# Eight experts in one straight line, with an expert's last products behind the next expert's first step

## The reference, cut to what matters

```
def moe_swiglu(h, router_w, w_in, w_out):          # h: 256 tokens x 1024
    logits = h @ router_w                           # 8 experts
    top_vals, top_idx = top_k(logits, 2)
    combine = sum(one_hot(top_idx) * softmax(top_vals))
    for e in range(8):                              # w_in[e]: 1024 x 7168, w_out[e]: 3584 x 1024
        g, u = split(h @ w_in[e], 2)
        out = out + combine[:, e] * ((silu(g) * u) @ w_out[e])
    return out
```

## Time and profile before

| | before |
|---|---|
| median of 3 runs | 2003.32 us (2002.88 to 2005.59) |
| profiled execution | 2006.99 us |
| its span, first to last instruction | 2004.9 us |
| PE busy | 1822.5 us, 91% |
| DVE / ACT busy | 474.2 us / 397.8 us |
| mean granted TensorE clock | 0.95 |

### The profile page before, as it was taken

How to read it: one execution, slowest core, us unless ns; L and a number is a source line. 1 busy time by engine, 2 the same in 40 slices (tenths; PEclk the granted TensorE clock), 3 DMA queues, 4 the chain that set the end, 5 groups by cost and what they waited for, 6 DMA issues and landing times.

```text
span 2004.9 us, 36376 instructions
## 1 busy us (share of the span) xinstructions
PE 1822.5 (91%) x16246; PEld 1078.4 (54%) x16246; DVE 474.2 (24%) x765; ACT 397.8 (20%) x671; POOL 34.9 (2%) x71
## 2 busy tenths in 40 slices
PE   5999889999999799757899998999989999999995
PEld 2744478888888588435445453443534434435343
DVE  3323454222333742644200101001010010010103
ACT  3233333222222521542001101010010100100001
POOL 1000100000000000010000000000000000000000
PEclk8998889999999899967899999999999999999997
DMA  9254452332233141547599898989989989899870
GB/s 374 87 207 170 125 170 76 105 97 93 102 113 110 55 139 43 213 157 296 210 373 340 340 378 314 371 325 343 393 314 349 366 321 388 307 348 373 313 307 23
DMA packets 141170, 477.63 MB, mean 238 GB/s; under 512 B 11168, under 2 KB 35096, under 8 KB 122576
## 3 DMA queue, kind: packets, MB, share of 16 engines
q1 hardware_dynamic: 137344, 467.64, 62.9%
q0 software_dynamic: 3664, 7.48, 1.2%
HBM read 473.96 MB, written 1.13 MB: 237 GB/s over the span
## 4 chain that ended last, share of the span: by engine, by line
PE 83%; DVE 8%; ACT 5%; issue 3%; DMA 1%; DVEq 0%; SPq 0%; ACTq 0%
PE ps L929 80%; DMA w_raw<-in_ada_w_dram 1%; DVE w_lo L1439 1%; PE ps L1353 1%; ACT p L815 1%; ACT w_hi L614 1%; DVE work L1503 1%; DVE row_max L1694 1%; PE ps L1101 1%; DVE residual L1526 1%; DVE work L1522 1%; DVE p L1713 0%; ACT work L630 0%; DVE p L1710 0%; ACT work L649 0%
## 5 line engine op out<-in xcount | busy, mean ns | idle before, releaser
L929 PE MATMUL ps<-w_hi,h_t 128*128 128x512 f32 (+1 forms) x960 | 298.2, 391 | 19.3 <-DVE h_t L1492 7.4
L929 PE MATMUL ps<-w_moe,h_te 128*32 128x256 f32 (+1 forms) x3072 | 259.2, 491 | 14.5 <-DVE residual L1835 14.5
L929 PE MATMUL ps<-w_raw,h_te 128*32 128x256 f32 (+2 forms) x4096 | 252.9, 406 | 0.0
L929 PE MATMUL ps<-h_t,w_hi 128*128 128x512 f32 (+1 forms) x768 | 222.0, 374 | 5.0 <-DVE h_t L1492 5.0
L1439 DVE TENSOR_TENSOR w_lo<-w_raw,w_hi 128x2048 fp32r<-128x2048 f32 x58 | 132.9, 2292 | 351.4 <-ACT w_hi L614 351.0
L929 PEld LDWEIGHTS ps<-w_hi,h_t 128*128 128x128 f32 x960 | 182.9, 193 | 60.2 <-issue 8.1
L929 PEld LDWEIGHTS ps<-w_raw,h_te 128*32 128x32 f32 x4096 | 130.6, 110 | 119.5 <-issue 69.7
L929 PEld LDWEIGHTS ps<-w_moe,h_te 128*32 128x32 f32 x3072 | 97.3, 111 | 168.3 <-issue 122.0
L929 PE MATMUL ps<-w_lo,h_t 128*128 128x512 f32 (+1 forms) x480 | 187.1, 390 | 0.0
L1834 DVE TENSOR_TENSOR residual<-silu_g,ps 128x512 f32<-128x512 f32 (+1 forms) x32 | 19.9, 621 | 660.9 <-ACT silu_g L886 660.9
L614 ACT ACTIVATE w_hi<-w_raw 128x2048 fp32r<-128x2048 f32 x58 | 110.8, 1914 | 328.9 <-PE ps L929 307.3
(11 more groups left out here) (233 smaller groups left out, 1265.1 us busy)
## 6 DMA issues: line engine op xcount, KB each, us to landing
w_moe<-in_expert_in_w_dram SPq DMA_DIRECT2D x96, 1024.0 KB, 5.8
w_raw<-in_expert_in_w_dram SPq DMA_DIRECT2D x64, 1024.0 KB, 6.9
w_raw<-in_ada_w_dram SPq DMA_DIRECT2D x48, 1024.0 KB, 5.6
w_raw<-in_expert_out_w_dram SPq DMA_DIRECT2D x48, 1024.0 KB, 6.7
w_moe<-in_expert_out_w_dram SPq DMA_DIRECT2D x48, 1024.0 KB, 7.7
work<-in_expert_in_w_dram SPq DMA_DIRECT2D x32, 1024.0 KB, 6.8
w_raw<-in_expert_in_w_dram SPq DMA_DIRECT2D x64, 512.0 KB, 6.1
w_raw<-in_ffn_in_w_dram SPq DMA_DIRECT2D x44, 512.0 KB, 4.9
```

Of the source, the lines that this page charges most:

```text
L929: return pe.matmul(out_, l, r, start=first, stop=last, skip_group_check=True)
```

## The change

Three things are done. (1) The list of blocks is now that of the whole round (`ROUND`): the eight in-0 blocks of the first expert (`HEAD`), then seven times a `CYCLE` that begins with in 1 and holds the next expert's in 0 ahead of the expert's own out 3, and a `LAST` cycle without it. SP, PE, ACT and DVE follow this order. (2) In round 0 the cycles are written out one after another on PE, ACT and DVE; SP keeps a loop (six turns). Rounds 1 and 2 keep loops on all engines. (3) The four `combine` products stand behind the blocks 4, 5, 6 and 7 of in 1, and the transposes of `onehot` for the next combine behind block 3 of out 0.

```diff
-EXPERT = [("in", 0, b) for b in range(8)]
+HEAD = step_blocks("in", 0)
+LAST = []
 for s_ in range(1, STEPS):
...
+    LAST += step_blocks("in", s_) + step_blocks("out", s_ - 1)
+CYCLE = LAST + step_blocks("in", 0, 1) + step_blocks("out", STEPS - 1)
+LAST = LAST + step_blocks("out", STEPS - 1)
+EB = len(CYCLE)
+ROUND = HEAD + CYCLE * (NE - 1) + LAST
...
@@ SP
-            with sp.Fori(0, NE - 1) as e:
-                for i in range(RING, EB):
-                    refill(rnd, e, i)
-                for i in range(RING):
-                    refill(rnd, e + 1, i)
-            for i in range(RING, EB):
-                refill(rnd, NE - 1, i)
+            with sp.Fori(0, NE - 2) as e:
+                for n in range(RING, EB + 8):
+                    refill(rnd, e, n, e)
+                for n in range(8, RING):
+                    refill(rnd, e + 1, EB + n, e)
+            for n in range(RING + EB * (NE - 2), len(ROUND)):
+                refill(rnd, (n - 8) // EB, n)
@@ ACT
+                silu(e, 3)
+                if not last:
+                    hte(NE * rnd + e + 2)
+                transposed(e, 3)
+                if not last:
+                    silu(e + 1, 0)
+                yhi(e, last)
+            hte(NE * rnd + 1)
+            silu(0, 0)
+            if rnd:
+                with act.Fori(0, NE - 1) as e:
+                    cycle(e)
+            else:
+                for e in range(NE - 1):
+                    cycle(e)
+            cycle(NE - 1, True)
@@ PE
-                    if (kind, s_, b) == ("in", 0, DK - 1):
-                        pe.wait_ge(y_lo, N + 1)
-                        for n, bank in enumerate((7, 5, 6)):
-                            combine(n, bank)
...
-                    if (kind, s_, b) == ("in", 1, 2):
-                        combine(3, 7)
...
+                    if kind == "in" and s_ == 1 and b >= 4:
+                        if b == 4:
+                            pe.wait_ge(y_lo, N + 1)
+                        if b == 5:
+                            pe.wait_ge(actt_ready, J + 1)
+                        if b == 7:
+                            pe.wait_ge(acc_done, N * 4 + 2)
+                        combine(b - 4, (7, 5, 6, 7)[b - 4])
...
-            with pe.Fori(0, NE) as e:
-                expert(e)
+            pe.wait_ge(hte_ready, NE * rnd + 1)
+            for n in range(8):
+                product(0, n, STEPS * NE * rnd)
+            if rnd:
+                with pe.Fori(0, NE - 1) as e:
+                    cycle(e)
+            else:
+                for e in range(NE - 1):
+                    cycle(e)
+            cycle(NE - 1, True)
@@ DVE
+                product(e, 3)
+                if not last:
+                    product(e + 1, 0)
                 ylo(e)
```

More of the change, by code:

```diff
@@ L61, with step_blocks @@
 N_RAW = B_MOE + ADA_BLOCKS
-EXPERT = [("in", 0, b) for b in range(8)]
+def step_blocks(kind, s_, ahead=0):
+    return [(kind, s_, b, ahead) for b in range(WIDTH[s_] // (128 if kind == "in" else 256))]
+HEAD = step_blocks("in", 0)
+LAST = []
 for s_ in range(1, STEPS):
[L64 to L70, removed]
+    LAST += step_blocks("in", s_) + step_blocks("out", s_ - 1)
[3 more added lines that the diff above has]
+ROUND = HEAD + CYCLE * (NE - 1) + LAST
+assert EB % RING == 0 and len(ROUND) == NE * EB
 assert GROUP * 3 == CAP
@@ L412, in ring, with moe_parts, moe_landed, count @@
         return WMOE[:, r - 2 - RAW, :]
[L414 to L425, removed]
+    def moe_parts(n):
+        return 2 if ROUND[n][:2] == ("in", STEPS - 1) else 1
+    def moe_landed(rnd, e, n):
+        def count(top):
+            return sum(16 * moe_parts(m) for m in range(n % RING, top, RING))
+        return rnd * count(len(ROUND)) + e * (count(8 + 2 * EB) - count(8 + EB)) + count(n + 1)
+    def moe_view(n):
+        kind, s_ = ROUND[n][:2]
         if kind == "out":
-            return ring(i).rearrange("p (j n) -> p j n", j=2)
+            return ring(n).rearrange("p (j n) -> p j n", j=2)
         if s_ < STEPS - 1:
-            return ring(i).rearrange("p (u n) -> p u n", u=2)
-        return ring(i).rearrange("p (k u n) -> p k u n", k=2, u=2)
+            return ring(n).rearrange("p (u n) -> p u n", u=2)
+        return ring(n).rearrange("p (k u n) -> p k u n", k=2, u=2)
     Z_BANK = (6, 3)
@@ L492, in experts @@
                 sp.wait_ge(scores, 16)
[L493 to L495 removed]
+                for n in range(RING):
+                    if 2 <= n < 2 + RAW:
+                        was, j = raw_order[N_RAW - RAW + n - 2]
                         if was == "w":
@@ L901, in yhi, with cycle @@
                 ins.then_inc(y_hi, 1)
-            hte(9 * rnd + 1)
-            with act.Fori(0, NE) as e:
-                silu(e, 0)
+            def cycle(e, last=False):
                 transposed(e, 0)
+                silu(e, 1)
+                transposed(e, 1)
                 act.wait_ge(ptt_ready, NE * rnd + e + 1)
                 act.activation(PTR[0:CAP, :], ps[0:CAP, 7, 0:2 * P], ACT.Copy).then_inc(pt_done, 1)
[L909 to L914, removed]
+                silu(e, 2)
+                transposed(e, 2)
+                silu(e, 3)
[14 more added lines that the diff above has]
+            cycle(NE - 1, True)
         experts(0)
@@ L1355, in transposes, with weights, product @@
                 ins.then_inc(tr_ready, 1)
[L1357 to L1361, removed]
+            def weights(e, n):
+                pe.wait_ge(w_landed[n % RING], moe_landed(rnd, e, n))
+                return moe_view(n)
+            def product(e, n, J):
+                kind, s_, b, ahead = ROUND[n]
+                if kind == "in":
+                    if b == 0:
+                        pe.wait_ge(act_done, FG + J + STEPS * ahead + s_)
+                    w = weights(e, n)
+                    if s_ < STEPS - 1:
+                        ins = in_block(b, w, WIDTH[s_])
+                    else:
+                        for k in range(2):
+                            ins = in_block(2 * b + k, w[:, k, :, :], WIDTH[s_])
+                else:
+                    if b == 0:
+                        pe.wait_ge(actt_ready, J + (s_ + 1))
+                    ins = out_block(s_, b, weights(e, n))
+                ins.then_inc(used, 1)
@@ L1362, in expert, with cycle @@
+            def cycle(e, last=False):
                 J = STEPS * NE * rnd + e * STEPS
                 N = 9 * rnd + e
[L1364 to L1372, removed]
-                        else:
[L1374 to L1377, removed]
+                at = len(ROUND) - len(LAST) if last else 8
+                for n in range(at, len(ROUND) if last else 8 + EB):
+                    kind, s_, b, ahead = ROUND[n]
+                    if (kind, s_, b) == ("in", 0, 0):
+                        pe.wait_ge(hte_ready, NE * rnd + e + 2)
+                    if (kind, s_, b) == ("out", 0, 0):
+                        pe.wait_ge(y_lo, N + 1)
+                    product(0 if last else e, n, J)
+                    if (kind, s_, b) == ("in", 1, 1):
+                        transposes(e, 0)
+                    if kind == "in" and s_ == 1 and b >= 4:
+                        if b == 4:
+                            pe.wait_ge(y_lo, N + 1)
+                        if b == 5:
[3 more added lines that the diff above has]
+                        combine(b - 4, (7, 5, 6, 7)[b - 4])
+                    if kind == "out" and s_ < STEPS - 1 and b == 1:
+                        if s_ == 0:
+                            pe.wait_ge(acc_done, N * 4 + 4)
+                        else:
@@ L1390, in expert @@
-                    if (kind, s_, b) == ("in", 1, 2):
-                        combine(3, 7)
-                    if (kind, s_, b) == ("in", 1, 4):
+                        if s_ == STEPS - 2 and not last:
+                            pe.wait_ge(hte_ready, NE * rnd + e + 2)
+                        transposes(e, s_ + 1)
+                    if (kind, s_, b) == ("out", 0, 3):
                         pe.wait_ge(acc_done, N * 4 + 5)
@@ L1396, in expert @@
                         ins.then_inc(ptt_ready, 1)
[L1397 to L1402, removed]
+                    if (kind, s_, b) == ("in", STEPS - 1, 3) and not last:
                         pe.wait_ge(actt_ready, J + STEPS - 1)
-                        gather(N + 2)
+                        gather(NE * rnd + e + 2)
             if rnd:
                 pe.wait_ge(acc_done, 36 * rnd + 1)
-            gather(9 * rnd + 1)
-            with pe.Fori(0, NE) as e:
-                expert(e)
+            gather(NE * rnd + 1)
+            pe.wait_ge(hte_ready, NE * rnd + 1)
[4 more added lines that the diff above has]
+                    cycle(e)
+            else:
+                for e in range(NE - 1):
+                    cycle(e)
+            cycle(NE - 1, True)
             pe.wait_ge(y_lo, 9 * rnd + 9)
```

68 lines of the change are left out of this document (36 added, 32 removed).

## The result

| | before | changed |
|---|---|---|
| median | 2003.1 us (2001.18 to 2005.59, 4 runs) | 1975.62 us (1972.87 to 1977.56, 4 runs) |
| ratio to before | | 0.9856, 95% interval 0.9843 to 0.9869 |
| span of the profiled execution | 2004.9 us | 1975.8 us |
| experts, first in 0 to the end of the last out 3 | 1014.2 us | 979.5 us |

The kernel is faster, by 27.5 us where 52 were forecast. The time lies outside the stated range of 1944 to 1968 us. Half of the mechanism came as predicted and half did not.

A forecast was written before the change was run, and what follows sets the result against it. PE's work, with loop turns, waits and slow clock, was taken as the bound. Eight experts of 119.7 us plus 2.2 and 1.7 us make 961.6 against 1014.2 us, a 52.6 us gain: 1951 us, range 1944 to 1968.

The forecast's parts named there:

- Part 1: PE's expert loop written out: seven turns go, with 28.4 us of gaps and 12.7 us of slow clock behind them.
- Part 2: Two out 3 blocks (5.3 us) cover the 2.2 us chain before in 1; wait gone for experts 1 to 7.
- Part 3: Moved copies and combines stay covered; single combines between in 1 blocks add 0.3 us per expert, 2.5 us in all.
- clean cycle of 119.4 us: PE's gapless work per expert: 96.96 us from in 1 through out 3, 20.78 for in 0, 1.66 for three combines.
- Part 4: SP's weight transfers in the expert stage: mean demand rises from 349 to 368 GB/s, costed at nothing.
- (b): Rival: weight transfers become the bound in the expert stage, with 349 GB/s as a ceiling; 1969 us, chance 8%.
- The first expert's slow clock of 1.7 us: Clock dip behind the first expert's 2.2 us wait at in 1, kept at 1.7 us; without it 1949 us.
- (a): Rival: the gap at PE's turn is not the loop's, so 28.4 + 12.7 us stay; 1992 us, chance 4%.

## Why the prediction was wrong

- **Part 1, straight line on PE: right.** 28.4 us of gaps became one of 0.4, and straight code stalls nowhere else. Three experiments carry it: PE alone written out gives 33 us, the same order with loops keeps 26.0 us of gaps, and the size of the body decides the price of the branch.
- **Part 2, out 3 behind in 0: this step failed.** It said that the wait "is gone for experts 1 to 7 with 3 us to spare" and, in part 3, that the blocks of the next silu "ended 5.3 us before". The cover was measured right (5.34 us), the chain nearly (2.04 us for 2.2), but I took from the order of the instructions that silu starts when its data are there. Its wait counts blocks, and the count held two more. Seven waits of 2.04 us, 14.3 us, stood again, and three of them brought a slow block, 5.1 us. The experiment that takes two from the count moved 21.4 us. The prediction had named the price of losing this cover, 2.2 us in each expert, but gave no chance to its being lost.
- **Part 3, the copies right, the single combines too cheap.** `y_lo`, the accumulations and `transposed` hold up nothing. The single combines were put at 0.3 us per cycle; PE's busy time is 0.65 us higher than in the old order written out (119.83 and 119.18 us). The cycle came out at 119.8 us for 119.7 all the same, and that is luck: the clean cycle of 119.4 us stood 0.2 us too high. It counted out 3 up to its end, but where no pause follows, the next block starts 0.2 us ahead of that end (1098.00 + 10.50 and 1108.32 above).
- **Part 4, the transfers: right.** 366 to 370 GB/s at a share of 0.97 to 0.98, rival (b) did not come.
- **Terms that I left out.** The new kernel has no `gather` in the last cycle, -3.7 us. Cycles of the changed kernel are 122.04 - 2.04 = 120.0 us long for 119.7 forecast, 2 us in all, and its first in 0 ran 1.3 us slow. The first expert's slow clock of 1.7 us, which I kept, did not come. With the 14.3 and 5.1 us that is 17.3 (14.3 + 5.1 - 3.7 + 2.0 + 1.3 - 1.7) of the 17.9 us between the stage's 979.5 us and the 961.6 forecast; 0.4 us more is the one "issue" wait.
- **Outside of the stage.** The experts began 3.4 us later than in before (969.47 for 966.12 us), behind unchanged code; over the kernels here this point lies between 961.55 and 969.56 us, so it tells of no edit. And the end became 2.2 us longer, which is shown in the last section.
- **Readings.** From slice 20 on the row of transfers shows 307 to 393 GB/s up to the last slice, not 291, and PE stands at 8 tenths in two slices. `h_te` is 15 us old at a turn, not tens. The chances of the forecast, (a) and (b) add up to 97%, not 96. None of this bears on the time.

Together: 17.9 + 3.4 + 2.2 = 23.5 us over the forecast span of 1952.3 us, which gives the 1975.8 measured. Rivals (a), 1992 us, and (b), 1969 us, both foresaw less gain, and the time fell between them, but neither cause was there. The case that happened, a cover that the order promises and a semaphore's count takes back, was not on my list of rivals at all, though the line stands in the diff's own functions.

## What to carry to other kernels

When work is moved past a place where another engine counts, every threshold of that count is part of the move: read the waits' numbers, not only the order, and look in the trace whether the waiting engine starts when its data are there or when something later ends. Two pauses at one place hide each other, so an edit that takes away one is worth less, and one that puts them together is worth more, than the sum says. PE's jump back took 0.2 us with a body of up to 1536 instructions and 3.4 to 6.3 us with 2048 and more, over all traces here; where a kernel has such a loop, try writing out that one engine first. It was 33 us here, of some 54 with all three. A pause of 1.8 us that is left can cost nearly as much again, 1.7 us, in slow clock.

## What the runs showed of the hardware

**Pauses of one length have two prices.** Pauses of 1.8 to 2.1 us on PE, all at the same place ahead of in 1, were followed by a first pair of blocks of 5.37 us in some cases and of about 7 us in others. It was slow 2 times of 8 in before, 3 of 8 in the changed kernel, 7 of 8 with PE alone written out, and never in the four of the kernels that have only one or two such pauses. Behind the eight pauses of 0.53 us it never was. What decides between the two was not found out.

**A jump forward can cost too.** At the end DVE jumps over rounds 1 and 2. The rows of before and of the changed kernel, both of DVE's timeline (start, duration, idle ahead):

```profile
1992.48 1.23 DVE L1884 CUSTOM_DVE_ANT_0 work<-y_acc 128x1024 f32<-128x1024 f32 x1 [1.60 <-issue]
```

```profile
1963.41 1.23 DVE L1937 CUSTOM_DVE_ANT_0 work<-y_acc 128x1024 f32<-128x1024 f32 x1 [3.84 <-issue]
```

DVE's branch over the rounds stands inside the pause, near its start, and takes the same time in both (before, then changed):

```profile
L1869 DVEq COMPARE_BRANCH  x1: 63/63/63, 1991.8 to 1991.8; - x1
```

```profile
L1922 DVEq COMPARE_BRANCH  x1: 72/72/72, 1960.5 to 1960.5; - x1
```

From the branch to the next work it is 0.7 us in before and 2.9 us in the changed kernel. The whole pause is 2.2 us longer, and it is 3.84 to 4.00 us in all four traces of the new order in straight line, 1.57 to 1.59 in the old order with all loops or PE's alone written out, and 1.60 in the new order with loops. The code that is jumped over is the same in the changed kernel and in its version with loops. So the length of that code alone doesn't decide it. Where the code lies in memory may, which was not tried.
